# The pooling layer's first block without its sample and meta columns, and a new order of the first loads

## The chip, the cores and the metric

The kernel runs on the 8 cores of one Trainium2 chip. Each core computes one of the 8 prompts and 16 of the 128 samples, without talking to the others. The metric is the device time of the slowest core in microseconds, as the median of several runs.

## The reference, cut to what matters

One inference step of a 2-layer model with 1024 channels. A prompt has 16 meta tokens and 2048 prompt tokens; a sample has one new token and stored state.

```python
for i in range(DEPTH):                       # 2 layers
    xn = rmsnorm(h, norm_mix[i])
    if i % 2 == 0:
        mix, buf = multiscale_pool_mix(xn, pool_prev, w_pool, pool_scale)
    else:
        mix, s = retention_mix(xn, ...)
    h = h + mix
    h = h + swiglu(rmsnorm(h, norm_ffn[i]), w_gate, w_up, w_down)
```

The pooling mixer has four groups of 256 channels with trailing windows of 2, 4, 8 and 16 tokens. For each token it takes the mean of the normed rows in the window (fewer at the sequence's start), subtracts the token's own normed row, multiplies by a 256x256 matrix of its group and scales each channel. For a sample the window reaches into 15 stored normed rows (`state_pool`); the last 15 rows are also an output.

## The kernel before, in words

Channels lie on the 128 partitions, in 8 channel tiles; tokens are columns. The first part of the program works on tile A with NA = 1056 columns: 16 samples (columns 0 to 15), 16 meta tokens (16 to 31) and 1024 prompt tokens. The other 1024 prompt columns are tile B and come later. The FFN computes on blocks of BW = 352 columns; `FIRST` cuts the first of these in two, so the pooling layer on A has four blocks: b = 0 (columns 0 to 175), 1 (176 to 351), 2 (352 to 703) and 3 (704 to 1055). Their four loads from `xT` are called x0 to x3 below (the list `xl`).

Each block of the pooling layer goes through these functions:

- `p0_norm(b)`: squares of 8 channel tiles (ScalarE, VectorE, GpSimd), summed by 8 matmuls with ones into the bank `sx`, then two ScalarE steps give 1/root (`rstd`, `rms_root`).
- `p0_x(b)`: VectorE writes the normed columns, as bf16 in tile B's room for channel tiles 0 to 5, as float32 in the room of the rotation tables (`XF`, in `cs_sb`) for tiles 6 and 7.
- `p0_group(b, g)`: pool minus token. For windows 2, 4 and 8 by matmuls that add shifted columns with scaled identities (`snb`), copied out by ScalarE; for window 16 by GpSimd additions in `cs_sb` and one VectorE operation each. Block 0 does this from column 32 on only.
- `p0_out(b, g)`: the 256x256 matmuls (`hB`, `wring`), VectorE's scaled addition onto tile A (`hadd`), and ScalarE's squares for the FFN's norm.
- `p0_f(b)`: the norm ahead of the FFN into `xn`.

`p0_meta` computes pool minus token of the meta columns on GpSimd. `p0_sample` sums the stored rows (`PV`, in tile C's room, named `hC` in the rows) by 32 float32 matmuls of 16 columns into the bank `po`, copies the sum to `prevsum`, and writes the samples' pool minus token. Both write columns that block 0's `p0_out` reads: in the kernel before, all 176 columns of block 0 go through it together.

The order on each engine is not the order of the source. Every call only enters an operation with what it depends on and an estimated cost into one list for the whole program. `Prog.arrange` then plans: it simulates the five engines with these costs and one shared transfer line, tries some 20 sets of priorities (8 of them with random changes from a fixed seed), and takes the order with the smallest simulated end. The source order enters through the dependencies, through which ring buffer an operation gets, and as a small part of the first priorities. The estimates that matter here: a float32 matmul counts 4 passes of at least 64 columns, a transfer has 300 bytes per ns and 3 us for landing. The chip runs each engine's list strictly in order, with waits on semaphores; a transfer issued by SyncE (`sp`) or GpSimd (`pool`) stands in that engine's list, and its `after` list makes the engine wait until those transfers have landed.

The weights go through a ring `wring` by transfers that GpSimd issues: number 0 is the pooling matrices, 1 to 4 are the first four FFN tiles (`w_gu`). `gate` gives the transfers that must have landed before weight 1, 2, 3 and 4 is issued. The FFN's first three weight tiles are used together, block by block (`n_outer=3`).

`nps_prev` copies 14 of the 15 stored rows of each sample from one DRAM tensor to an output. `cf2` is a part of the constants that only the retention layer reads.

## Time and profile before

| what | value |
|---|---|
| time, median of 3 runs | 1647.43 us (1644.41 to 1648.02) |
| the profiled execution | 1646.35 us |
| its span, slowest core (core 7) | 1644.7 us |
| spans of all cores | 1629.8 to 1644.7 us |
| TensorE busy | 1581.0 us (96%) |
| VectorE, ScalarE, GpSimd busy | 885.0, 665.3, 610.2 us |

All rows and stretches are of core 7. PE is TensorE's matmuls, PEld its weight loads, DVE is VectorE, ACT ScalarE, POOL GpSimd, SP SyncE. L721 is the line of the matmul helper, L730 that of tensor-tensor operations, L733 of scalar-tensor-tensor ones, L741 of activations: one line stands for many places, so the tile names tell them apart. The granted clock (PEclk) is a share of TensorE's full 2.4 GHz.

### The profile page before, as it was taken

How to read it: one execution, taken by the hardware profiler on the slowest of the kernel's cores; microseconds unless marked ns; L12 is line 12 of the kernel's file. 1: busy time of each engine (PE TensorE's matmuls, PEld its weight loads, DVE VectorE, ACT ScalarE, POOL GpSimd, SP SyncE). 2: the span in 40 equal slices, each digit the busy share in tenths (PEclk: the TensorE clock that was granted, in tenths of full speed). 3: DMA queues.
4: the chain of work that ended last, by engine and by line, in shares of the span. 5: the costliest groups of instructions: out<-in, count | busy, mean ns of one | idle time of the engine just before them, and what ended most of it. 6: DMA issues, size and time to landing. Idle time of an engine off the chain costs nothing.

```text
span 1644.7 us, 32433 instructions; the slowest of 8 cores (1629.8 to 1644.7 us)
## 1 busy us (share of the span) xinstructions
PE 1581.0 (96%) x10775; PEld 1002.9 (61%) x10775; DVE 885.0 (54%) x1650; ACT 665.3 (40%) x1174; POOL 610.2 (37%) x921
## 2 busy tenths in 40 slices
PE   5899999999999998999999999999999999999996
PEld 4666666555565555666666666665555655666665
DVE  4822222855656782888374444576567657422225
ACT  5511022354433763444374535465454445220124
POOL 5300002557847671222140111134588578000014
PEclk9999999999999999999999999999999999999998
DMA  8544344243236568475769998967533331544413
GB/s 211 107 70 86 68 75 77 52 78 65 51 66 142 106 179 211 103 180 148 169 163 222 219 246 222 222 177 216 152 73 78 78 65 27 116 78 79 80 35 105
DMA packets 55746, 201.30 MB, mean 122 GB/s; under 512 B 6688, under 2 KB 21024, under 8 KB 45840
## 3 DMA queue, kind: packets, MB, share of 16 engines
q0 software_dynamic: 15840, 103.82, 37.4%
q1 hardware_dynamic: 39600, 95.07, 17.1%
q8 instruction: 90, 1.47, 0.4%
q14 instruction: 72, 0.59, 0.1%
q10 hardware_dynamic: 144, 0.35, 0.1%
HBM read 256.69 MB, written 47.25 MB: 185 GB/s over the span
## 4 chain that ended last, share of the span: by engine, by line
PE 85%; DMA 5%; DVE 3%; POOL 2%; issue 2%; ACT 1%; DVEq 0%; SPq 0%; POOLq 0%; ACTq 0%
PE pb L721 77%; PE po L721 3%; DMA nrs<-U 2%; DMA U<-sret 2%; PE psU L721 2%; PE sx L721 2%; PE sx L725 1%; DMA hC<-sp_prev 1%; PE psU L1299 1%; POOL accb L730 0%; DVE U L733 0%; DVE hB L733 0%; PE po L1337 0%; POOL aff L730 0%; ACT L741 0%
## 5 line engine op out<-in xcount | busy, mean ns | idle before, releaser
L721 PE MATMUL pb<-xn,wring 128*128 128x352 bf16 (+3 forms) x5856 | 914.8, 308 | 14.5 <-DVE hC L730 7.9
L721 PEld LDWEIGHTS pb<-xn,wring 128*128 128x128 bf16 x5856 | 562.4, 98 | 308.1 <-issue 28.3
L721 PE MATMUL pb<-hC,wring 128*128 128x352 bf16 (+4 forms) x2576 | 411.3, 305 | 2.1 <-DVE hB L730 1.9
L730 DVE TENSOR_TENSOR hC<-pb,sg 128x352 bf16<-128x352 f32 (+3 forms) x270 | 136.3, 508 | 352.1 <-PE pb L721 341.9
L721 PEld LDWEIGHTS pb<-hC,wring 128*128 128x128 bf16 x2576 | 245.7, 98 | 123.6 <-issue 8.9
L741 ACT ACTIVATE sg<-pb 128x352 bf16<-128x352 f32 (+3 forms) x270 | 120.6, 451 | 471.7 <-PE pb L721 454.8
L721 PE MATMUL pb<-wring,xn 128*128 128x512 bf16 (+1 forms) x544 | 155.1, 379 | 0.0
L157 POOL DMA_DIRECT2D wring<-w_gu x44 | 24.6, 560 | 313.3 <-PE pb L721 311.3
L730 POOL TENSOR_TENSOR accb<-accb,sq 128x352 f32<-128x352 f32 (+2 forms) x108 | 94.4, 874 | 81.1 <-ACT sq L741 57.4
L730 DVE TENSOR_TENSOR hB<-pb,hB 128x352 f32<-128x352 f32 (+4 forms) x152 | 73.3, 494 | 81.2 <-PE pb L721 79.1
L730 DVE TENSOR_TENSOR hA<-pb,hA 128x352 f32<-128x352 f32 (+1 forms) x144 | 72.4, 512 | 68.8 <-PE pb L721 68.3
L733 DVE SCALAR_TENSOR_TENSOR U<-psU,ksf,U 128x512 f32<-128x512 f32 x120 | 88.4, 746 | 23.1 <-DMA U<-sret 15.3
L733 DVE SCALAR_TENSOR_TENSOR U<-U,psU 128x1024 f32<-128x1024 f32 x64 | 78.0, 1218 | 24.2 <-PE psU L721 13.1
L1240 ACT ACTIVATE on<-po,stt 128x512 bf16<-128x512 f32 x68 | 52.9, 777 | 94.2 <-POOL stt L1234 47.2
L157 POOL DMA_DIRECT2D wring<-w_d x32 | 17.3, 541 | 187.8 <-PE pb L721 187.6
L730 POOL TENSOR_TENSOR aff<-aff,cf_sb 128x512 f32<-128x512 f32 (+1 forms) x68 | 67.5, 993 | 47.3 <-DVE aff L730 47.1
L737 ACT CAST U<-U 128x1024 bf16<-128x1024 f32 x64 | 66.7, 1043 | 36.5 <-DVE U L733 26.6
L737 ACT CAST snb<-U 128x1024 bf16<-128x1024 f32 x60 | 62.2, 1039 | 46.8 <-DVE U L733 39.0
L721 PEld LDWEIGHTS pb<-wring,xn 128*128 128x128 bf16 (+1 forms) x544 | 51.2, 98 | 48.0 <-issue 6.7
L1229 DVE BATCH_NORM_STATS2 stt<-po 128x6 f32<-128x512 f32 x68 | 47.4, 697 | 41.4 <-PE po L721 21.4
L730 DVE TENSOR_TENSOR aff<-sx,cf_sb 128x512 f32<-128x512 bf16 (+1 forms) x80 | 46.9, 586 | 37.7 <-PE sx L725 18.4
L741 ACT ACTIVATE sq<-hB 128x352 bf16<-128x352 f32 (+2 forms) x98 | 46.4, 486 | 48.5 <-DVE hB L730 19.8
(155 smaller groups left out, 1680.1 us busy)
## 6 DMA issues: line engine op xcount, KB each, us to landing
wring<-w_gu POOLq DMA_DIRECT2D x44, 1024.0 KB, 10.5
U<-sret SPq DMA_DIRECT2D x60, 512.0 KB, 6.5
nrs<-U SPq DMA_DIRECT2D x60, 512.0 KB, 9.0
wring<-w_in POOLq DMA_DIRECT2D x24, 1024.0 KB, 10.5
wring<-w_d POOLq DMA_DIRECT2D x16, 768.0 KB, 9.0
wring<-w_d POOLq DMA_DIRECT2D x16, 640.0 KB, 11.1
wring<-w_out POOLq DMA_DIRECT2D x8, 1024.0 KB, 10.0
hA<-xT SPq DMA_DIRECT2D x2, 1408.0 KB, 14.8
```

Source lines behind the costliest of these rows:

```text
L157: h.dma_start(out=o_ap, in_=i_ap).then_inc(sem, 16)
L721: return P.op('pe', lambda h: h.matmul(out, lhsT=lhsT, rhs=rhs, start=start, stop=stop), reads=reads, writes=writes, cost=passes * max(_fr ...
L725: return P.op('pe', lambda h: h.transpose(out, in_, ident), reads=reads, writes=writes, cost=max(_free(out), 64) / 2.4 + 1.3)
L730: return P.op(eng, lambda h: h.tensor_tensor(out=out, in0=a, in1=b, op=op), reads=reads, writes=writes, cost=cost)
L733: return P.op('dve', lambda h: h.scalar_tensor_tensor(out=out, in0=a, scalar=s, in1=b, op0=op0, op1=op1), reads=reads, writes=writes, cost ...
L737: return P.op('act', lambda h: h.copy(out=out, in_=in_), reads=reads, writes=writes, cost=130 + 0.93 * _free(out))
L741: return P.op('act', lambda h: h.activation(out=out, in_=in_, func=func, bias=bias, scale=scale), reads=reads, writes=writes, cost=160 + 0 ...
L1229: dve(lambda h: h.bn_stats(out=s[0:n, 0:6], in_=po[0:n, :]), [pok], [sk], 690)
L1240: act(lambda h: h.activation(out=on[0:n, :], in_=po[0:n, :], func=ACT.Identity, bias=s[0:n, 9:10], scale=s[0:n, 8:9]), [pok, sk], [onk], 777)
L1299: ins = e.matmul(psU[:, i, :], lhsT=identb[p, 32 * i + b + i:32 * i + b + i + 1].to_broadcast([32, 128]), rhs=vx[h][p, :], start=True, sto ...
```

## The change

Block 0's `p0_out` leaves out columns 0 to 31. A new function `p0_late` treats them for all 8 channel tiles together, once the sample and meta parts are there. The blocks' source order becomes norm, next norm, block, with the sample part, the late columns and the FFN's norms of blocks 0 and 1 behind block 1. The stored rows are loaded behind x1's landing and not ahead of x1, x3 behind x2's landing; weight 1 waits for the stored rows, weight 2 for x3, weights 3 and 4 for weights 1 and 2. The second part of the constants and the copy `nps_prev` follow the rotation tables' load. One `rstd` (block 2's) lives in `accb`, as four are held at once.

```diff
         xl = [load_x(A, FIRST[0][0], *FIRST[0])]
-        pvl = P.dma('sp', [(PV[:, 0, :], sp_prev[0:128, :]), (PV[0:112, 1, :], sp_prev[128:240, :])], writes=pvk, semkey='pv')
         xl.append(load_x(A, FIRST[1][0], *FIRST[1]))
-        xl.extend([load_x(A, c0, c0, n, after=xl[0:1]) for (c0, n) in FIRST[2:]])
-        gate.update({1: xl[1:2], 2: xl[2:3], 3: xl[3:4], 4: xl[3:4]})
+        xl.append(load_x(A, FIRST[2][0], *FIRST[2], after=xl[0:1]))
+        pvl = P.dma('sp', [(PV[:, 0, :], sp_prev[0:128, :]), (PV[0:112, 1, :], sp_prev[128:240, :])], writes=pvk, semkey='pv',
+                    after=xl[1:2])
+        xl.append(load_x(A, FIRST[3][0], *FIRST[3], after=xl[2:3]))
+        gate.update({1: [pvl], 2: xl[3:4], 3: [1], 4: [2]})
         w_issue()
-        cf2l = P.dma('sp', [(cf[:, NCF1:NCF], cfd[:, NCF1:NCF])], writes=['cf2'], after=xl[3:4])
-        P.dma('sp', [(nps_prev[:, :, :], sp_prev.rearrange("(b j) d -> b j d", j=15)[:, 1:15, :])],
-              semkey='o_npsprev', is_out=True, after=[cf2l])
...
-            pw[b] = rms_stats(c0, n)
+            pw[b] = rms_stats(c0, n, buf=(accB[0], 'accb') if b == 2 else None)
...
         def p0_sample():
-            nrows(xs[:], ['xs'], 0, 0)
...
+        def p0_late(wp, wk):
+
+            pb, pk = PO.take()
+            for cm in range(8):
+                g, m = cm // 2, cm % 2
+                for kc in range(2):
+                    mm(pb[:, cm * 32:(cm + 1) * 32], wp[:, g, kc, m * 128:(m + 1) * 128], B.b(2 * g + kc, 1, 0, 32), kc == 0, kc == 1,
+                       wk + B.bk(2 * g + kc, 1, 0, 32), [pk])
+            tmp = aff[:].rearrange("p a b -> p (a b)")[:, 0:256].rearrange("p (c n) -> p c n", c=8)
+            ak = [k for c in range(8) for k in A.fk(c, 0, 32)]
+            h32 = A.f3()[:, 0:8, 0:32]
+            tt('dve', tmp, pb[:, 0:256].rearrange("p (c n) -> p c n", c=8), bc_n(cf[:, C_PS:C_PS + 8], 32), ALU.mult,
+               [pk, 'cf'], ['aff'])
+            PO.free()
+            tt('dve', h32, h32, tmp, ALU.add, ak + ['aff'], ak)
+            aact(xn[:, 0:8, 0:32], h32, ACT.Square, ak, [k for c in range(8) for k in xk(c, 0, 32)])
+
         def p0_out(b, g, wp, wk):
             c0, n = FIRST[b]
+            if b == 0:
+                c0, n = 32, n - 32
...
         p0_norm(0)
+        nrows(xs[:], ['xs'], 0, 0)
         p0_meta()
+        p0_norm(1)
+        p0_block(0)
+        p0_norm(2)
+        p0_block(1)
+        p0_norm(3)
         p0_sample()
-        for b in range(last + 1):
-            if b < last:
-                p0_norm(b + 1)
-            else:
-                nrows(halo[:], [('halo', c) for c in range(8)], 1040, last)
-            p0_block(b)
-            if b < last:
-                p0_f(b)
-            else:
-                norm_soon(A, C_NF0, b, FIRST[b][0], FIRST[b][1], 'F00')
+        p0_late(wp, wk)
+        p0_f(0)
+        p0_f(1)
+        p0_block(2)
+        nrows(halo[:], [('halo', c) for c in range(8)], 1040, last)
+        p0_block(3)
+        p0_f(2)
+        norm_soon(A, C_NF0, last, FIRST[last][0], FIRST[last][1], 'F00')
         wrel(wprec)
-        P.dma('sp', [(cs[:, 0, :], csd[0, :, 0:NA]), (cs[:, 1, :], csd[1, :, 0:NA])], writes=csk, semkey='cs')
+        csl = P.dma('sp', [(cs[:, 0, :], csd[0, :, 0:NA]), (cs[:, 1, :], csd[1, :, 0:NA])], writes=csk, semkey='cs')
+        cf2l = P.dma('sp', [(cf[:, NCF1:NCF], cfd[:, NCF1:NCF])], writes=['cf2'], after=[csl])
+        P.dma('sp', [(nps_prev[:, :, :], sp_prev.rearrange("(b j) d -> b j d", j=15)[:, 1:15, :])],
+              semkey='o_npsprev', is_out=True, after=[cf2l])
```

## Rows read from the trace of the kernel before

**Rows 1.** The page's first part: busy time, share of the span, instructions.
```profile
PE 1581.0 (96%) x10775; PEld 1002.9 (61%) x10775; DVE 885.0 (54%) x1650; ACT 665.3 (40%) x1174; POOL 610.2 (37%) x921
```

**Rows 2.** Stretches of the span: length, each engine's busy time, granted clock, transfers.
```profile
0.00:80.00 80.00, 56.83 (x448) 42.38 (x448) 53.35 (x115) 44.50 (x120) 40.09 (x79) 0.96 0.76 163
80.00:400.00 320.00, 318.70 (x2090) 200.27 (x2091) 129.71 (x238) 84.40 (x163) 89.00 (x122) 1.00 0.39 69
```

**Rows 3.** Stretches inside the first 81 us; columns PE, PEld, DVE, ACT, POOL.
```profile
9.40:16.40 7.00, 1.33 (x8) 0.84 (x8) 4.49 (x11) 2.52 (x9) 3.39 (x6) 1.00 1.02 233
16.40:24.80 8.40, 8.03 (x43) 8.06 (x44) 0.00 (x0) 0.96 (x5) 3.21 (x11) 1.00 1.03 332
24.80:66.40 41.60, 34.92 (x242) 21.45 (x240) 39.41 (x80) 31.28 (x87) 29.10 (x47) 0.92 0.85 148
...
67.60:80.80 13.20, 11.34 (x147) 10.99 (x145) 8.72 (x21) 6.61 (x15) 0.00 (x0) 1.00 0.18 66
```

**Rows 4.** Timelines of TensorE, then ScalarE: start, length, idle before and releaser.
```profile
16.77 6.98 PE L721 MATMUL po<-cf_sb,hC 128*128 128x16 f32 x32 [4.85 <-DMA hC<-sp_prev]
...
62.92 0.46 PE L721 MATMUL pb<-xn,wring 128*128 128x176 bf16 x4
...
67.62 8.60 PE L721 MATMUL pb<-xn,wring 128*128 128x176 bf16 x111
...
23.84 0.27 ACT L737 COPY prevsum<-po 128x128 f32<-128x128 f32 x1 [10.97 <-PE po L721]
24.00 1.78 ACT L741 ACTIVATE xn<-hA 128x176 bf16<-128x176 f32 x7
```

**Rows 5.** Timeline of VectorE.
```profile
24.81 0.98 DVE L733 SCALAR_TENSOR_TENSOR hB<-prevsum,xs 128x32 bf16<-128x32 f32 x4 [8.48 <-POOL prevsum L730]
26.77 0.77 DVE L733 SCALAR_TENSOR_TENSOR hA<-pb,cf_sb,hA 128x176 f32<-128x176 f32 x2 [0.97 <-PE sx L721]
27.78 0.40 DVE L733 SCALAR_TENSOR_TENSOR hB<-hA,w,rstd 128x176 bf16<-128x176 f32 x1 [0.24 <-ACT rstd L741]
```

**Rows 6.** The chain of work that ended last, in order of time.
```profile
2.17 14.36 DMA hC<-sp_prev
```

**Rows 7.** Stretches of 2 us, columns as in rows 2.
```profile
38.00:40.00 2.00, 0.00 (x0) 0.00 (x0) 2.00 (x6) 1.53 (x6) 2.00 (x4) 1.00 1.44 266
...
46.00:48.00 2.00, 2.00 (x8) 1.03 (x7) 2.00 (x4) 0.85 (x2) 0.94 (x1) 0.50 1.01 164
```

**Rows 8.** First loads: kind, median to landing; x1's issue; x2's and x3's.
```profile
wring<-wpool POOLq DMA_DIRECT2D x1, 512.0 KB, 13.0
...
L157 SPq DMA_DIRECT2D hA<-xT x1: 1039/1039/1039, 2.6 to 2.6; - x1
...
DMA to landing us min/median/max: 15.7/15.7/15.7
...
L157 SPq DMA_DIRECT2D hA<-xT x2: 1723/3320/4917, 9.5 to 11.3; - x2
...
DMA to landing us min/median/max: 13.6/14.8/16.0
```

**Rows 9.** Groups by shape on VectorE: count, busy us, mean ns, idle before.
```profile
L733 DVE SCALAR_TENSOR_TENSOR hA<-pb,cf_sb,hA 128x176 f32<-128x176 f32 x16 | 5.8, 392 | 1.0 <-PE sx L721 1.0
...
L730 DVE TENSOR_TENSOR qm<-qsf,cf_sb 128x256 bf16<-128x256 f32 x8 | 4.3, 541 | 0.3
```

**Rows 10.** Weights 1 and 2 to 4, issued by GpSimd: starts, us to landing.
```profile
L157 POOL DMA_DIRECT2D wring<-w_gu x1: 596/596/596, 27.9 to 27.9; - x1
...
DMA to landing us min/median/max: 17.9/17.9/17.9
...
L157 POOL DMA_DIRECT2D wring<-w_gu x3: 535/550/591, 39.0 to 40.1; - x3
...
DMA to landing us min/median/max: 15.3/19.2/24.3
```

**Rows 11.** Timeline of SyncE: the rotation tables' issue.
```profile
64.23 0.82 SPq L157 DMA_DIRECT2D cs_sb<-cs  x2
```

More of the change, by code:

```diff
@@ L805, in square, with rms_root @@
             return o, ok
-        def rms_root(pb, pk, n):
-            r, rk = rstdR.next()
+        def rms_root(pb, pk, n, buf=None):
+            r, rk = buf if buf else rstdR.next()
             first = aact(r[:, 0:n], pb[:, 0:n], ACT.Ln, [pk, 'epsb'], [rk], bias=epsb[:, 0:1])
@@ L830, in last_sum, with rms_stats @@
             tt('pool', out, x[0], x[1], ALU.add, x[2], outk)
-        def rms_stats(c0, n, tiles=range(8)):
+        def rms_stats(c0, n, tiles=range(8), buf=None):
             bank = SX
@@ L836, in rms_stats @@
                 mm(pb[:, 0:n], onesb[:], xn[:, c, c0:c0 + n], c == tiles[0], c == tiles[-1], ['onesb'] + xk(c, c0, n), [pk])
-            out = rms_root(pb, pk, n)
+            out = rms_root(pb, pk, n, buf)
             bank.free()
```

## The prediction

> **What bounds the kernel now.** I read the page first. TensorE is busy 96% of the span [rows 1], so the change can only give back what TensorE loses. The stretches show where that is: 23.2 us idle in the first 80, and 63.7 - 23.2 = 40.5 us spread over the other 1564.7 [rows 1, 2]. The change lies wholly in the first stretch, and the next 320 us have only 1.3 us to spare.
>
> Next I read the engines' timelines through the first 80 us, to see which engine sets the pace. From 24.8 to 66.4 us VectorE is busy 39.4 of 41.6 us while TensorE has gaps [rows 3]: there the pooling layer runs at VectorE's pace. From 16.4 to 24.8 us VectorE does nothing. The reason is on two other timelines. The sample part's 32 float32 matmuls wait 4.85 us for the stored rows and run 16.77 to 23.75 us; every pooling matmul of block 0 stands behind them in TensorE's list. ScalarE waits 10.97 us for the same matmuls to copy their result, and the squares of block 1 stand behind that copy [rows 4, 5]. The chain that ended last agrees: it begins with 14.36 us of the stored rows' transfer and goes on through the float32 matmuls [rows 6].
>
> So there are two things to lose in this stretch: a VectorE gap of 8.48 us before the sample's small operation at 24.81, and then nearly two more until block 0's first output addition at 26.77 [rows 5].
>
> A caution on the clock: after TensorE had 0.00 busy from 38 to 40 us, the granted clock reads 0.50 in three stretches of 2 us up to 48, TensorE's 1.2 GHz level; the last of them stands in the rows. But VectorE is busy 2.00 of 2.00 us there [rows 7], so the low clock has cover and I price its removal at nothing. If that cover went, half of the 6 us, 3 us, would be to gain.
>
> **Part 1: block 0 without the sample and meta columns.** Its output additions no longer wait for the sample matmuls or GpSimd's meta sums. Block 0's normed columns end on VectorE where its gap begins, at 24.81 - 8.48 = 16.33 [rows 5]. The pooling weights are in at 1.9 + 13.0 = 14.9 us [rows 8]. TensorE waits idle for the stored rows up to 16.77 [rows 4], so block 0's outputs can follow the normed columns directly. Eight of them at 392 ns [rows 9] are 3.1 us: VectorE is then at about 19.5 at the latest, in place of a start of these additions at 26.77.
>
> **Part 2: the stored rows behind block 1's and block 2's columns.** Landing times: x1 was issued at 2.6 and landed 15.7 later, at 18.3. x2 and x3 were issued at 9.5 and 11.3 and landed 13.6 and 16.0 later, at 23.1 and 27.3 [rows 8]. The stored rows are 0.98 MB ahead of x1; at the 233 GB/s of 9.4 to 16.4 us [rows 3] that is 4.2 us, so x1 lands at about 14. From its first square at 24.00 to its first normed column at 27.78 block 1 took 3.8 us [rows 4, 5]. These columns can begin at 18, while block 0's additions end, against 27.78 before. x2 now goes ahead of the stored rows and lands near 19; they land near 22; x3, issued when x2 has landed, comes in near 27 as before, because the bytes before it are the same. So x2 is there 4 us earlier than before, and block 2's work stands behind all of block 1's.
>
> Here a rule speaks against the change. The trace first: the same link moved 332 GB/s from 16.4 to 24.8 with all loads queued behind one another [rows 3]; the new waits issue the stored rows after x1 has landed and x3 after x2. If nothing else is in flight, each such wait empties the link. The Trainium skill (DMA: Bandwidth & Descriptors, "Anatomy of one DMA") gives each transfer a fixed part of about 2 us, mostly the receipt before the semaphore moves. By it two waits would cost 4 us of the link if nothing overlapped. The rows show the cover: by the landing times above x2 is in flight during the first wait and the stored rows during the second, so I price both at nothing. An x3 at 31 would still be ahead of its use, as some 14 us of VectorE work on block 1's and block 2's columns and block 0's norm lie between 18 and it.
>
> **Part 3: what is added.** `p0_late` puts two operations of 128x256 on VectorE, at most 541 ns each by the nearest row [rows 9], together 1.1 us; block 0's eight additions lose 32 of their 176 columns each, at most 8 x 392 x 32/176 = 0.6 us back, and as an operation has a fixed part I take half. Net +0.8 us on VectorE. Its 16 matmuls of 32 columns and one Square of 256 lie on engines with gaps: nothing. Using `accb` for one root and moving the sample's normed rows on GpSimd cost nothing, as GpSimd is busy 29.1 of 41.6 us [rows 3].
>
> **Part 4: the float32 matmuls in their new place.** They are still 7.0 us of TensorE, 218 ns each [rows 4], and now stand in the stretch where VectorE is full. The planner's cost for one is 4 x 64/2.4 + 1.3 = 108 ns, so it takes them for 3.5 us: up to 3.5 us are not planned for. Lower bound 0: VectorE has normed columns to make meanwhile. Upper bound 7.0, if VectorE runs dry for all of it. I take 2, nearer to 0, because block 1's eight normed columns alone are about 3 us of VectorE work that needs no matmul.
>
> **Part 5: later loads and gates.** The constants and the stored rows' copy to the output leave the time of the first weights' loads and follow the rotation tables, issued at 64.23 [rows 11]. The link is then at 66 GB/s [rows 3], while 0.5 + 0.9 MB no longer compete with the weights. Weight 1 landed at 27.9 + 17.9 = 45.8 us, weight 2 at 39.0 + 15.3 = 54.3 and weight 3 near 39.6 + 19.2 = 58.8 us [rows 10], and the first FFN matmul ran at 62.92 [rows 4]. With 1.4 MB less and a start some 6 us earlier they can be in by 53 to 57: enough for an FFN start at 57. On SyncE nothing but those two transfers waits behind the tables; the sync queue is empty for that time. I price it at nothing. The gate of weight 3 on weight 1, however, is a wait in GpSimd's list; behind it stand the window sums of channels 6 and 7, and behind these VectorE and TensorE.
>
> **The sum.** Gap removed 8.5 us, additions +0.8, float32 block +2: 5.7 us, and I round to 6. Nothing downstream absorbs it: from 67.6 to 80.8 TensorE is busy 11.3 of 13.2 us, and from 80 to 400 it is 318.7 of 320 [rows 2, 3], so what comes earlier stays earlier. The profiled execution took 1646.35 us (span 1644.7 and 1.65 around it), 1.1 under the median of 1647.43. So its like would be 1640.4 and the median 1641.4.
>
> **Rivals.**
> *A, a late weight takes the gap's place (slower).* Weight 3 may be issued only when weight 1 has landed, weight 4 when weight 2 has. Before, three issues went out together from 39.0 to 40.1. If weight 1 goes at 28 as before and takes its 17.9 us, weight 3 goes at 46 and, with 15 to 24 us to land [rows 10], arrives at 61 to 70. Above 63 us it decides: the FFN starts later than before. At 67 the kernel would be 4 us slower, 1651. Against it: the first one's 17.9 us were shared with loads that are moved away. The planner's own belief of 10 us for a weight, though, makes a stall of the GpSimd list possible. Chance 0.16.
>
> *B, TensorE's gaps fill too.* With weights in by 45, block 0's 96 FFN matmuls (7.4 us, by 111 of them in 8.60 us [rows 4]) could run in gaps, of which TensorE has 6.7 us from 24.8 to 66.4 [rows 3]. If most of them fill, some 6 us more are gained: 1635.5. For it: no low clock from idle time either. Against: the VectorE product and ScalarE's table loads come along. Chance 0.16.
>
> *C, it makes no difference.* The gap moves: TensorE's float32 block starves VectorE for the full 7.0 us, leaving 8.5 - 0.8 - 7.0 = 0.7 us; or the order is planned anew over the whole program and returns the gain, somewhere in the 40 us that TensorE idles after 80. Time 1646.7. Chance 0.18.
>
> The remaining 0.50 is the forecast, 1641.4, its own range 1638.5 to 1644.
>
> **From this to the numbers.** A difference of 0.2%, 3.3 us, is what a measurement of this kernel can tell from none. Faster: forecast (0.45 of its 0.50), B 0.16 and a little of C, 0.63. Same: most of C and edges, 0.20. Slower: A, and a new order that is worse elsewhere, 0.17. The range reaches to B's time with the float32 block at its lower bound, 1634, and to A's with a smaller stall, 1650.
>
> **What will show it.** Right, if VectorE's gap from 16.3 to 24.8 shrinks to under 2 us, block 0's additions begin before 18, the float32 matmuls stand after 21, the first FFN matmul comes before 58 and VectorE's dense stretch ends near 61. Wrong in part 2, if the squares of block 1 begin after 17. Rival A shows as TensorE or GpSimd waiting on a weight; C as a VectorE gap beside the float32 matmuls, or TensorE idle time after 80 us grown by 3 us or more; B as more than 8 us less idle before 80. The prediction fails if a different engine than VectorE sets the pace from 25 to 60 us.

## The result, and the profile after

The changed kernel took 1655.34 us (median of 7 runs; the kernel before 1647.43 us on the same chip). The ratio is 1.0046, 95% interval 1.0035 to 1.0057: 0.46% or some 8 us slower, where 6 us faster was forecast. In some executions of every version the cores of a die show a lower granted clock and the time is 1 to 17% longer; medians here are over all executions, ratios leave these out. The profiled execution has core 5 as its slowest, with a span of 1653.8 us.

The page's first part after, for [rows 1]:

```profile
PE 1584.7 (96%) x10791; PEld 1005.9 (61%) x10791; DVE 884.3 (53%) x1652; ACT 665.9 (40%) x1175; POOL 610.4 (37%) x921
```

Stretches of core 5 after, for [rows 2]:

```profile
0.00:80.00 80.00, 54.17 (x432) 40.58 (x432) 50.98 (x113) 43.32 (x117) 40.71 (x79) 0.98 0.68 159
80.00:400.00 320.00, 317.38 (x2085) 200.79 (x2085) 127.79 (x237) 83.21 (x160) 84.79 (x118) 0.99 0.35 68
400.00:600.00 200.00, 198.65 (x1319) 118.74 (x1318) 126.46 (x229) 98.51 (x164) 133.58 (x198) 1.00 0.47 108
600.00:660.00 60.00, 54.88 (x357) 34.75 (x355) 31.97 (x52) 31.00 (x56) 19.65 (x31) 0.94 0.80 196
660.00:1000.00 340.00, 333.49 (x2312) 215.35 (x2311) 217.49 (x409) 154.02 (x238) 78.70 (x135) 1.00 0.75 183
1000.00:1200.00 200.00, 193.80 (x1281) 116.49 (x1279) 117.41 (x217) 104.83 (x158) 66.63 (x97) 0.99 0.74 184
```

The same stretches of core 7 before, behind its first two, which are [rows 2]:

```profile
400.00:600.00 200.00, 197.27 (x1311) 117.55 (x1310) 129.11 (x234) 97.63 (x165) 132.94 (x196) 1.00 0.50 105
600.00:660.00 60.00, 51.31 (x334) 32.78 (x332) 26.14 (x44) 27.73 (x51) 17.40 (x28) 0.94 0.88 199
660.00:1000.00 340.00, 333.80 (x2312) 214.80 (x2309) 214.37 (x404) 154.37 (x239) 78.56 (x135) 1.00 0.73 179
1000.00:1200.00 200.00, 197.17 (x1315) 120.03 (x1316) 119.77 (x220) 106.26 (x161) 66.39 (x95) 1.00 0.79 199
```

Take TensorE's idle time in each (length less busy). Up to 1000 us it is 23.2 + 1.3 + 2.7 + 8.7 + 6.2 = 42.1 us before and 25.8 + 2.6 + 1.4 + 5.1 + 6.5 = 41.4 us after. The matmuls done by then are 6,495 and 6,505, of which 16 are `p0_late`'s. So the two are level at 1000 us, although the changed stretch is the first 80. The difference shows from there on: 2.8 against 6.2 us of idle time in the next 200, where the change touches no operation.

**What stands in that place.** VectorE's timeline on core 5 after:

```profile
1118.44 1.59 DVE L733 SCALAR_TENSOR_TENSOR U<-psU,ksf,U 128x512 f32<-128x512 f32 x2
1124.92 1.61 DVE L733 SCALAR_TENSOR_TENSOR U<-psU,ksf,U 128x512 f32<-128x512 f32 x2 [4.88 <-DMA U<-sret]
1126.44 0.95 DVE L730 TENSOR_TENSOR hA<-pb,cs_sb 128x352 f32<-128x352 f32 x2
```

TensorE's, of the same time:

```profile
1121.36 1.89 PE L721 MATMUL pb<-wring,xn 128*128 128x512 bf16 x8
1127.54 3.57 PE L721 MATMUL pb<-wring,xn 128*128 128x512 bf16 x8 [4.28 <-DVE hA L730]
```

And stretches of 4 us (columns as in rows 2):

```profile
1124.00:1128.00 4.00, 0.46 (x2) 0.22 (x3) 2.98 (x5) 1.29 (x2) 0.90 (x2) 0.95 0.52 182
1128.00:1132.00 4.00, 4.00 (x15) 1.33 (x14) 4.00 (x7) 1.53 (x3) 2.21 (x4) 0.63 0.87 308
```

`U<-psU,ksf,U` updates a sample's retention state, which SyncE has loaded from `sret`. The load is late, VectorE waits 4.88 us in front of it, and the products `hA<-pb,cs_sb` that TensorE's banks wait for stand behind it in VectorE's list. TensorE loses 4.28 us, then the granted clock reads 0.63 over 4 us, and eight matmuls take 3.57 us where eight alike had just taken 1.89. SyncE's waits of 1095 to 1150 us tell why the load is late:

```profile
SPq L357 <- ACT U L741: 33.2, 8, 10.0
SPq L357 <- DMA nrs<-U: 22.4, 5, 13.9
```

Each state buffer goes load, update, store, load. The next load waits for the store of the state before it (`nrs<-U`), and the store for ScalarE's last step on it. In the kernel before (core 7) SyncE waits there too, but its longest wait for a store is 5.7 us and not 13.9, and VectorE never waits for `sret`:

```profile
SPq L357 <- DMA nrs<-U: 18.0, 5, 5.7
```

On the other cores after, VectorE's wait near 1120 us is 3.4 (core 0), 1.0 (3) and 3.0 us (7) and none is listed on the rest. Core 3, with a span of 1652.1 us, meets the same chain at its next place (VectorE's timeline, TensorE's, and a stretch of 4 us):

```profile
1165.73 0.29 DVE L730 TENSOR_TENSOR U<-sx,cf_sb 128x128 bf16<-128x128 f32 x1 [5.16 <-DMA nrs<-U]
```
```profile
1166.17 0.58 PE L721 MATMUL po<-hC,U 128*128 128x512 bf16 x1 [4.49 <-DVE U L730]
```
```profile
1164.00:1168.00 4.00, 1.83 (x8) 1.00 (x9) 0.29 (x1) 0.47 (x1) 2.20 (x4) 0.50 0.32 122
```

**The last matmuls.** TensorE's waits there, first after, then before:

```profile
1637.21 1.13 PE L721 MATMUL pb<-hC,wring 128*128 128x160 bf16 x14 [1.96 <-DVE hB L730]
1638.53 1.96 PE L721 MATMUL pb<-hC,wring 128*128 128x160 bf16 x26 [0.19 <-DVE hB L730]
```
```profile
1628.21 3.21 PE L721 MATMUL pb<-hC,wring 128*128 128x160 bf16 x40 [1.20 <-DVE hB L730]
```

Another 0.8 + 0.2 us is lost there, and on cores with a low clock behind that gap more. The first gap is 1.96 or 1.97 us on all eight cores after, and 1.20 to 1.22 on all eight before.

**The start.** VectorE's timeline after, for [rows 5]:

```profile
12.22 1.13 DVE L730 TENSOR_TENSOR xn<-hA 128x176 bf16<-128x176 f32 x3 [5.81 <-DMA hA<-xT]
15.13 0.88 DVE L733 SCALAR_TENSOR_TENSOR cs_sb<-hA,w,rstd 128x160 f32<-128x160 f32 x2 [1.79 <-ACT rstd L741]
...
24.01 0.64 DVE L733 SCALAR_TENSOR_TENSOR hA<-pb,cf_sb,hA 128x144 f32<-128x144 f32 x2 [3.02 <-POOL cs_sb L730]
...
34.55 0.40 DVE L733 SCALAR_TENSOR_TENSOR hA<-pb,cf_sb,hA 128x176 f32<-128x176 f32 x1 [5.45 <-PE pb L721]
```

TensorE's, for [rows 4]:

```profile
22.83 0.84 PE L721 MATMUL sx<-xn,onesb 128*128 128x352 bf16 x2 [4.12 <-ACT xn L741]
...
26.64 0.44 PE L721 MATMUL po<-cf_sb,hC 128*128 128x16 f32 x2
...
34.46 1.41 PE L721 MATMUL po<-cf_sb,hC 128*128 128x16 f32 x8
...
66.52 0.24 PE L721 MATMUL pb<-xn,wring 128*128 128x176 bf16 x1
```

ScalarE's, where x2 is waited for:

```profile
22.19 0.88 ACT L741 ACTIVATE xn<-hA 128x352 bf16<-128x352 f32 x2 [3.02 <-DMA hA<-xT]
22.98 0.80 ACT L737 CAST hB<-pb 128x144 bf16<-128x144 f32 x4
```

The loads, for [rows 8] and [rows 10], each line of issues above its time to landing: x2 alone, the stored rows, weights 2 to 4:

```profile
L157 SPq DMA_DIRECT2D hA<-xT x1: 368/368/368, 12.2 to 12.2; - x1
...
DMA to landing us min/median/max: 9.9/9.9/9.9
...
L157 SPq DMA_DIRECT2D hC<-sp_prev x2: 341/546/751, 14.5 to 14.9; - x2
...
DMA to landing us min/median/max: 9.6/10.2/10.8
...
L157 POOL DMA_DIRECT2D wring<-w_gu x3: 591/591/591, 43.3 to 56.3; - x3
...
DMA to landing us min/median/max: 7.9/9.2/11.5
```

The gap of 8.48 us at 16.3 is gone, as forecast; three take its place, at 21 us (3.02), at 29 us (5.45) and 5.81 instead of 3.32 us in front of the first squares. The profile names GpSimd for the one at 21 us; the product that VectorE needs there begins on TensorE only at 23.49, behind block 2's sums (the row at 22.83). In the stretch that was VectorE's dense one, it is now busy 32.55 us and not 39.41:

```profile
24.80:66.40 41.60, 34.69 (x238) 24.21 (x236) 32.55 (x67) 24.87 (x69) 26.44 (x43) 0.96 0.66 135
```

The first FFN matmul is at 66.52 us on this core, against 61.66 on the same core before. Over the eight cores it stands at 60.4 to 67.0 us (61.2 to 63.9 before): three cores are 1.6 to 3.4 us earlier, three 4.5 to 5.8 us later, two level. No core has the 57 us that was forecast.

**Slow and fast neighbours.** The same core number is not the same case in two executions. In 197 of the 229 executions that enter the ratios of this document, the four longest spans belong to one core of each pair of neighbours (0 and 1, 2 and 3, 4 and 5, 6 and 7). In the profile before these are 1, 2, 4 and 7, and x0 lands later on them from the start: VectorE's first squares begin at 9.5 to 11.6 us there and at 8.5 to 8.8 on the others. Core 5 was the faster of its pair before and is the slower one after. By this sorting the first FFN matmul comes at 62.9 to 63.9 us on the slower cores before and at 62.6 to 67.0 after, on the faster ones at 61.2 to 62.0 and 60.4 to 63.5. What the two cores of a pair share was not tested.

### The profile page after: what moved, and what is told of

It is laid out like the page before. It is cut to its first block, busy times and chain, and to the rows that moved or that the text cites. A ratio compares the mean times of both kernels' runs of the same rounds, so it can differ in the third digit from the quotient of the medians.

```text
span 1653.8 us, 32463 instructions; the slowest of 8 cores (1636.1 to 1653.8 us)
## 1 busy us (share of the span) xinstructions
PE 1584.7 (96%) x10791; PEld 1005.9 (61%) x10791; DVE 884.3 (53%) x1652; ACT 665.9 (40%) x1175; POOL 610.4 (37%) x921
## 4 chain that ended last, share of the span: by engine, by line
PE 82%; DMA 7%; DVE 3%; POOL 3%; issue 2%; ACT 2%; DVEq 0%; POOLq 0%; SPq 0%; ACTq 0%
PE pb L721 74%; DMA U<-sret 3%; PE po L721 3%; DMA nrs<-U 3%; PE psU L721 2%; PE sx L721 1%; PE sx L725 1%; DMA hA<-xT 1%; DVE xn L733 1%; PE psU L1316 0%; ACT on L1257 0%; POOL aff L730 0%; DVE U L733 0%; DVE hA L730 0%; DVE hB L733 0%
## 5 line engine op out<-in xcount | busy, mean ns | idle before, releaser
L721 PEld LDWEIGHTS pb<-hC,wring 128*128 128x128 bf16 x2576 | 246.0, 98 | 126.2 <-issue 11.5
L721 PE MATMUL pb<-wring,xn 128*128 128x512 bf16 (+1 forms) x544 | 161.3, 383 | 4.7 <-DVE hA L730 4.3
L730 POOL TENSOR_TENSOR accb<-accb,sq 128x352 f32<-128x352 f32 (+2 forms) x108 | 93.6, 866 | 60.2 <-ACT sq L741 40.9
L721 PEld LDWEIGHTS pb<-wring,xn 128*128 128x128 bf16 (+1 forms) x544 | 51.9, 98 | 55.9 <-issue 13.1
L721 PE MATMUL pb<-hB,wring 128*128 128x352 bf16 (+3 forms) x256 | 60.7, 309 | 4.5 <-DVE hA L733 3.2
L741 ACT ACTIVATE U<-U 128x1024 f32<-128x1024 f32 x60 | 63.1, 1055 | 4.0
## 6 DMA issues: line engine op xcount, KB each, us to landing
wring<-w_d POOLq DMA_DIRECT2D x16, 640.0 KB, 10.8
```

The source lines that it names most:

```text
L721: return P.op('pe', lambda h: h.matmul(out, lhsT=lhsT, rhs=rhs, start=start, stop=stop), reads=reads, writes=writes, cost=passes * max(_fr ...
L730: return P.op(eng, lambda h: h.tensor_tensor(out=out, in0=a, in1=b, op=op), reads=reads, writes=writes, cost=cost)
L741: return P.op('act', lambda h: h.activation(out=out, in_=in_, func=func, bias=bias, scale=scale), reads=reads, writes=writes, cost=160 + 0 ...
```

## The experiments

The start is what the change edits. The 13,961 operations from the first FFN on are the same in both kernels, but `arrange` plans both parts in one go, and it put them in another order: 3,797 of TensorE's 10,367 places, 462 of VectorE's 1,546, 278 of ScalarE's 1,038 and 45 of SyncE's 168 differ. On these last three engines most lie in the FFN of tile B (operations 7103 to 9256 of the common ones) and the second retention layer (9257 to 11947), where the stall was found; of TensorE's, 1,382 lie ahead of 7103. So the first pair swaps these orders. The form of all such kernels: `arrange` is run as it is, and then, on each engine, the places of the common operations from LO to HI are filled with these operations in the donor's order (`TAIL`, whose unpacking is left out here; LO is 0 and HI 13961 in the first pair).

```diff
-        for i in best[1]:
-            self.ops[ops[i].eng].append(ops[i])
+        n0 = n - 13961
+        lists = [[i for i in best[1] if self.eng[i] == e] for e in range(len(ENGS))]
+        for e, mine in enumerate(TAIL):
+            it = iter([i for i in mine if LO <= i < HI])
+            lists[e] = [next(it) + n0 if LO <= i - n0 < HI else i for i in lists[e]]
```

**e1_new_start_old_rest**: the changed kernel, common operations in the order of the kernel before.

> The changed kernel in its first 561 operations (the whole pooling layer's source), but every engine runs the 13961 operations behind them in the order of the kernel before. Theory 'two losses' (the start loses some 4 us, the order planned anew for the rest loses another 4): 1651, about +0.25%. Theory 'the start alone': as the changed kernel, 1655. Theory 'the order alone': 1647 or below. In the profile of the slowest core the first FFN matmul stays at 65 to 67 us in any case.

**e2_old_start_new_rest**: the kernel before, common operations in the changed kernel's order.

> The mirror image: the first 542 operations of the kernel before in their old order, and behind them the changed kernel's order of the common 13961. Theory 'two losses': 1651. 'The start alone': 1647.4, no change. 'The order alone': 1655.

Measured: e1 0.9992 (0.998 to 1.0004), 1647.94 us; e2 1.0059 (1.0036 to 1.0081), 1657.74 us. The loss goes with the order, and the start without it is worth nothing that can be measured.

**e5_new_but_second_half** and **e6_new_but_first_half**: the changed kernel with the old order for common operations 7103 to 13960 alone, and for 0 to 7102 alone.

> The changed kernel, but the operations from the second half's first FFN on (source positions 7103 to 13961 of the common part) stand in the old kernel's order among themselves; everything ahead of them keeps the new order. Theory 'the second half's order costs the time, by a state load that VectorE waits for in front of the rotation products near 1120 us': within 0.15% of the kernel before. Rival 'the loss is spread over the whole of the new order': half of it, +0.25%.

> The complement: the changed kernel with the first half's operations behind the start (positions 0 to 7103) in the old order, the second half in the new one. Theory 'second half': slower by 0.4 to 0.6%, as the changed kernel. Rival 'spread': +0.25%. In the profile VectorE should wait some 5 us for a state load near 1120 us.

Measured: e5 1.0001 (0.999 to 1.0011), e6 1.0039 (1.0027 to 1.0052). The order of the second half carries it; TensorE's 1,382 other places in the first half cost nothing that can be measured.

**e7_old_start_seed3** and **e8_new_start_seed3**: is it the change that makes the planner's order bad, or is it luck? Only the seed of the planner's random priorities is altered, in the kernel before (e7) and in the changed one (e8).

```diff
-        rng = np.random.default_rng(1)
+        rng = np.random.default_rng(3)
```

> The kernel before, nothing changed but the seed of the planner's random tries (3 in place of 1). The order that comes out for the common part differs from the changed kernel's in only some 150 places, and from its own old one in some 4700. Theory 'the measured loss has nothing to do with what the change does, the planner just settled on its other order': +0.5%, 1655. Rival 'the loss comes from the new start': no change.

> The changed kernel with the planner's seed 3: a third order, unlike both. If the choice of order is a matter of luck of some 0.5%, this falls anywhere from -0.2 to +0.6% against the kernel before; the state-load wait near 1120 us decides which. If the start were what costs, it would be at +0.46% as the changed kernel.

Measured: e7 1.0055 (1.0042 to 1.0068), 1657.46 us; e8 0.9998 (0.9988 to 1.0008), 1648.80 us. e7 is the unchanged kernel. Its new plan differs from the changed kernel's in only some 150 places, and it has the same loss and the same mark in VectorE's waits of 1095 to 1150 us:

```profile
DVE U L733 <- DMA U<-sret: 5.4, 1, 5.4
DVE hA L730 <- PE pb L721: 3.0, 3, 2.2
```

e6 has the first at 6.1 and e2 at 5.9 us on their slowest cores; e1 and e5 have none there. e8's plan is a third order, unlike both (7,094 of TensorE's places differ from the changed kernel's, 6,956 from the old ones), and as good as the old one. So the slow order comes with the old start too, and a good one with the new start.

The planner itself gives simulated ends of 1583.8 us for the kernel before, 1587.6 for the changed one, 1585.3 for e7 and 1583.5 for e8. In the changed kernel and in e7 the order taken is one that its fixed turns reach before any random try, and no random try beat it. In the kernel before and in e8 a random try did. So the good order of the kernel before was a find of the random tries, and the changed kernel fell back to the other kind. The planner ranks these four as the chip does, but sees 0.1 to 0.3% between the kinds where the chip shows 0.5%.

**e3_f32_cost**: e1, with the planner told twice the time for a float32 matmul.

```diff
-            passes = 4 if rhs.dtype == F32 else 1
+            passes = 8 if rhs.dtype == F32 else 1
```

> As the first of these, but the planner is told that a float32 matmul of 16 columns takes 215 ns (8 passes in its formula) and not 108; it plans the pooling layer anew, the rest keeps the old order. Theory 'the float32 block starves VectorE, because it is planned at half its length': VectorE's gap of 5.45 us among block 0's and block 1's additions falls below 3 us and the time to about 3 us under the first of these. Rival 'the late loads set the start': within 1.5 us of it.

**e4_old_loads**: e1, with the first loads and gates of the kernel before; the constants and the copy stay late.

```diff
         xl = [load_x(A, FIRST[0][0], *FIRST[0])]
+        pvl = P.dma('sp', [(PV[:, 0, :], ...), (PV[0:112, 1, :], ...)], writes=pvk, semkey='pv')
         xl.append(load_x(A, FIRST[1][0], *FIRST[1]))
-        xl.append(load_x(A, FIRST[2][0], *FIRST[2], after=xl[0:1]))
-        pvl = P.dma('sp', [(PV[:, 0, :], ...), (PV[0:112, 1, :], ...)], writes=pvk, semkey='pv', after=xl[1:2])
-        xl.append(load_x(A, FIRST[3][0], *FIRST[3], after=xl[2:3]))
-        gate.update({1: [pvl], 2: xl[3:4], 3: [1], 4: [2]})
+        xl.extend([load_x(A, c0, c0, n, after=xl[0:1]) for (c0, n) in FIRST[2:]])
+        gate.update({1: xl[1:2], 2: xl[2:3], 3: xl[3:4], 4: xl[3:4]})
```

> As the first of these, but with the loads in the order of the kernel before: stored rows between x0 and x1, x2 and x3 behind x0's landing, the weights' gates as before; the two late transfers stay late. The new source order of the blocks stays. Theory 'x1 right behind x0 shares the link with it, and the stored rows share it with x2': x0 lands near 9.5 us again in place of 10.6 to 12.2, and the time is 2 to 4 us under the first of these. Rival 'the float32 block alone': no change against it. What I predicted for the change, 6 us under the kernel before, would show here if the loads alone spoiled it: 1641.

Measured: e3 0.9995 (0.9981 to 1.0009), e4 1.0029 (1.0015 to 1.0043). A truer cost of the float32 matmuls brings nothing in time, although VectorE's gap at 29 us shrinks from 5.44 us on e1's slowest core to 1.45 on e3's. The new loads are worth something: without them the new source order is 0.3% slower than before, with them level (the planner orders the start anew in e4, so this is the loads together with their plan). The first FFN matmul of e4 stands at 65.3 to 68.0 us on all cores. Block 1's normed columns then stand behind the float32 matmuls (VectorE's timeline of e4):

```profile
22.97 2.29 DVE L874 SCALAR_TENSOR_TENSOR hB<-hA,w,rstd 128x176 bf16<-128x176 f32 x4 [4.32 <-PE po L862]
```

**e10_no_f32_block**: e1, with the 32 float32 matmuls replaced by one bf16 matmul of 128 columns with the same wait for the stored rows. It leaves out the sums over the stored rows.

```diff
-            for c in range(8):
-                g = c // 2
-                for kc, kn in ((0, 128), (1, 112)):
-                    off = C_AW + (kc * 4 + g) * 16
-                    mm(pb[:, c * 16:(c + 1) * 16], PV[0:kn, kc, c * 128:(c + 1) * 128], cf[0:kn, off:off + 16],
-                       kc == 0, kc == 1, pvk + ['cf'], [pk])
+            mm(pb[:, 0:128], onesb[:], identb[:], True, True, pvk + ["onesb", "identb"], [pk])
```

> New start, old order behind it, and the 32 float32 matmuls over the stored rows are replaced by one bfloat16 matmul of 128 columns with the same wait for the stored rows: the sums over the stored rows are left out. It shows what the block costs in the start, and whether time saved there reaches the end. Theory 'the block starves VectorE by some 5 us': the first FFN matmuls come 4 to 6 us earlier than with the block, and the time falls by the same, to 1643. Rival 'a stretch paced by the state transfers, near 640 us, takes up what the start gives': the start is earlier, the time within 2 us of the one with the block. Rival 'the block is hidden': neither.

Measured: 1.0000 (0.9974 to 1.0027). The first FFN matmul comes at 59.7 to 61.4 us on all cores, where e1 has 60.4 to 67.8: on three cores some 6 us are gained at the start, and the time doesn't show them. Carried to the end, 6 us under e1 would be 0.9956, outside the interval; a part of up to 3 us would lie inside it.

**e11_x1_behind_x0**: e1, with x1 issued once x0 has landed.

```diff
-        xl.append(load_x(A, FIRST[1][0], *FIRST[1]))
+        xl.append(load_x(A, FIRST[1][0], *FIRST[1], after=xl[0:1]))
```

> New start, old order behind it, and x1 is issued only when x0 has landed, so that x0 has the queue alone. Theory 'x1 right behind x0 shares the link and makes x0 2 us late': x0 lands at 8 to 9.5 us in place of 10.6 to 12.2, block 0's normed columns come 2 us earlier, and the time falls by 1 to 2 us or not at all, if x1's own lateness takes it back. Rival 'x0 is late for another reason': it lands where it did.

Measured: 0.9988 (0.9975 to 1.0001). x0 did not land earlier for it: VectorE's first squares start at 10.9 to 13.2 us on the cores, in e1 at 10.9 to 12.4, before at 8.5 to 11.6. That x0 is slowed by x1 beside it has fallen. What does go with x0 is where GpSimd's list has the pooling matrices' load (`wring<-wpool`). In the kernel before and in e2 it is issued at 1.95 us, and the squares begin at 8.5 to 11.6 us. In e7, where SyncE's first loads are the same and in the same order, the plan has it ahead of two small memory fills, at 1.59 us, and the squares begin at 10.2 to 14.4; so it is in the changed kernel and in e4 (1.56 us; 10.8 to 13.1 and 11.0 to 12.6). The first line is of before, the second of e7:

```profile
1.94 0.71 POOL L157 DMA_DIRECT2D wring<-wpool  x1 [0.42 <-issue]
```
```profile
1.59 0.71 POOL L157 DMA_DIRECT2D wring<-wpool  x1 [0.33 <-issue]
```

No run moves this load alone, so that it is the cause is not shown.

**e9_one_step_later**: the changed kernel's own order, with the state update in front of which VectorE waited, its TensorE and ScalarE parts and its load moved by hand to where the old order has them, behind the rotation's products.

```diff
-        for i in best[1]:
-            self.ops[ops[i].eng].append(ops[i])
+        lists = [[i for i in best[1] if self.eng[i] == e] for e in range(len(ENGS))]
+        n0 = n - 13961
+        for e, who, behind in ((0, (9092,), 9340), (0, (9284,), 9465), (2, (9093, 9094, 9095, 9096), 9329),
+                               (1, (9136, 9137, 9188, 9189), 9420), (4, (9091,), 9090)):
+            l = [i for i in lists[e] if i - n0 not in who]
+            at = l.index(behind + n0) + 1
+            lists[e] = l[:at] + [i + n0 for i in who] + l[at:]
```

> The changed kernel as it was planned, but one pair of sample steps is moved to where the old order has it: two broadcasts on TensorE, four state updates on VectorE, their four copies on ScalarE, and one state load ahead of two stores on SyncE, all to behind the rotation products of the same head. Nothing else moves. Theory 'VectorE stands for a state load in front of the rotation products, and that costs': the wait of up to 4.9 us near 1120 us is gone and the time falls by 3 to 6 us against the changed kernel, to 1649 to 1652. Rival 'the wait is only a symptom, the state transfers are late all through the new order': it comes back at the next load, 1655.

Measured: 1.0080 (1.0063 to 1.0098), slower still. The wait near 1120 us shrank to 0.3 to 1.7 us, on seven cores, and came back at the next place: TensorE waits 5.4 to 6.5 us for VectorE there on every core. VectorE's waits on e9's core 3 from 1150 to 1200 us:

```profile
DVE U L737 <- DMA nrs<-U: 6.8, 1, 6.8
```

**e12_new_short_stores** and **e13_old_rest_short_stores**: the stores of the sample states of heads 2 and 3 move 128 of 1024 columns, in the changed kernel with its own order (e12) and in e1 (e13). The planner is told the full size, so the orders stay. Both leave out the rest of these stores.

```diff
-                    P.dma('sp', [(nrs[b, h], t)], reads=k, semkey=('sst', i), is_out=True)
+                    m = 1024 if u < 32 else 128
+                    P.dma('sp', [(nrs[b, h][:, 0:m], t[:, 0:m])], reads=k, semkey=('sst', i), is_out=True).cost = 524288
```

> The changed kernel's own order, but the sample states of heads 2 and 3 are stored only in their first 128 of 1024 columns: 32 of 64 stores move an eighth of their bytes, and the rest of these outputs is left out. Theory 'the new order of the second half runs short of transfer time there': VectorE's wait for a state load near 1120 us goes and the loss with it, to 1647 or less. Rival 'the new order costs compute time of its own': still slower than the next kernel by 6 us or more.

> New start, old order behind it, with the same short stores. Theory 'transfer time': no more than 2 us under the kernel with full stores (1648), so that the two orders come within 2 us of each other. Rival 'compute': the distance between the orders stays at 7 us.

Measured: e12 1.0036 (1.0022 to 1.005), e13 0.9997 (0.9983 to 1.0012). VectorE's wait for `sret` is gone on every core of e12 (0.2 us at most), yet e12 stays 0.39% behind e13. TensorE's busy time from 1000 to 1300 us tells how much came back; one line each of before (core 7), e1 (core 4), after (core 5), e7 (core 3) and e12 (core 2), their slowest cores:

```profile
1000.00:1300.00 300.00, 295.34 (x1987) 179.23 (x1988) 188.14 (x348) 151.63 (x232) 142.81 (x210) 1.00 0.61 151
```
```profile
1000.00:1300.00 300.00, 294.39 (x1980) 178.37 (x1979) 187.87 (x347) 151.32 (x233) 142.61 (x209) 1.00 0.60 150
```
```profile
1000.00:1300.00 300.00, 290.25 (x1937) 174.44 (x1935) 180.11 (x334) 148.57 (x229) 138.56 (x204) 0.99 0.61 147
```
```profile
1000.00:1300.00 300.00, 284.53 (x1884) 170.10 (x1883) 174.56 (x324) 144.91 (x224) 138.42 (x202) 0.98 0.60 144
```
```profile
1000.00:1300.00 300.00, 293.32 (x1971) 177.59 (x1970) 182.68 (x339) 149.54 (x230) 139.52 (x207) 1.00 0.50 114
```

Idle: 4.7 and 5.6 us with the old order, 9.8 and 15.5 with the new one, 6.7 with the new one and short stores. So the state transfers are most of what core 5 loses in this stretch, and e12 loses in other places. VectorE's lists tell where. From its last operation among the common ones up to 6300 to its last among those up to 11947, e12 takes 573.7 to 574.0 us on all eight cores, where e13 takes 571.9 to 572.1 on seven (and the changed kernel 574.6 to 580.8). So 1.8 us stay whatever the stores move. From there to the end of the span e12 takes 243.7 to 244.0 us on six cores and e13 241.6 on all: another 2.1. Of the end, e12's core 2 has the gap of after and then a low clock (26 matmuls in 3.50 us, in 1.96 after):

```profile
1635.11 1.13 PE L844 MATMUL pb<-hC,wring 128*128 128x160 bf16 x14 [1.97 <-DVE hB L853]
1636.42 3.50 PE L844 MATMUL pb<-hC,wring 128*128 128x160 bf16 x26 [0.19 <-DVE hB L853]
```

**e14_old_ffn** and **e15_old_ret**: the changed kernel with the old order for common operations 7103 to 9099 alone, and from 9100 on alone.

> The changed kernel with the operations 7103 to 9100 of the common part (the second half's first FFN and the state steps among it, up to head 2) in the old order. Theory 'the loss is made in this FFN, where the state transfers fall behind': within 0.15% of the kernel before. Rival 'it is made in the retention part behind it': +0.4%.

> The complement: operations 9100 to 13961 (the second retention part and the last FFN) in the old order, all else the changed kernel's. Theory 'the FFN': +0.4%. Rival 'the retention part': within 0.15% of the kernel before.

Measured: e14 1.0070 (1.0054 to 1.0086); e15 1.0058 (1.0036 to 1.0080), from two executions only. Both theories fell: neither half of the good order takes the loss away, and e14 is slower than the changed kernel (1.0046). The loss can't be put down to one of the halves. That an order's FFN part and its retention part belong together would fit; it is not shown.

**e16_both**: e1 with the edits of e3 and e11.

> The changed start with the operations behind it in the order of the kernel before, x1 issued once x0 has landed, and the planner told 8 passes for a float32 matmul. The theory that the order behind the start carries the loss, and that the start's own gain is absorbed near 600 us: the two edits each measured 0.9988 and 0.9995 of the kernel before, so together 0.998 to 0.9995, about 1645 us. The rival, that the float32 block and the gaps of the start still cost VectorE some us that would count: 0.996 or lower, under 1641 us. If the first FFN matmul comes earlier than in the start-only run on the slow cores and the time stays, the first theory holds again.

Measured: 0.9984 (0.9974 to 0.9994), 1645.35 us against 1648.67. The first FFN matmul is at 60.2 to 62.0 us on all cores, so no core is late any more. It is the only one of the sixteen experiments whose interval lies wholly under 1: 2.6 us, at the edge of what can be told, and under the 3.3 us that the prediction itself asks for.

## Why the prediction was wrong, point by point

**The step that failed** is the sum's "Nothing downstream absorbs it [...] so what comes earlier stays earlier", for two reasons. The larger: the order of the rest was taken as given. Rival C named a new plan for the whole program, but let it do no more than return the gain, and "a new order that is worse elsewhere" shared 0.17 with rival A, which alone had 0.16. The new plan measured 1.0046 - 0.9992 = 0.54%, or 8.9 us (e1 against after), and 0.55% with no change of the start at all (e7). A mechanism that moves a third of TensorE's list deserved a range of its own, on both sides.

The other reason: a lead or a lag at the start is evened out near 600 us. Up to 600 us TensorE idles 23.2 + 1.3 + 2.7 = 27.2 us before and 25.8 + 2.6 + 1.4 = 29.8 after; from 600 to 660 us it is 8.7 against 5.1. Before, one wait of TensorE behind `hC` holds 6.7 us of this, at the time when SyncE stores sample states and loads the next (TensorE's timeline before, then SyncE's waits from 590 to 680 us):

```profile
647.18 16.21 PE L721 MATMUL pb<-xn,wring 128*128 128x352 bf16 x94 [6.68 <-DVE hC L730]
```
```profile
SPq L357 <- DMA nrs<-U: 25.3, 3, 16.8
```

The cores drift apart in this place. VectorE's 1100th operation from the end starts at 573.3 to 576.0 us on the eight cores before, its 1000th from the end at 665.5 to 678.3. In e1, with the same order behind the start, the slowest core is 4.6 us behind the slowest one of before at the first of these (579.7 against 575.1) and 1.4 behind at the second (679.7 against 678.3). That e10's 6 us of start don't show in the time fits this. That the transfers are what evens it out was read from the rows and not tested by itself.

**A step ahead of it failed too.** The sum's first line, "Gap removed 8.5 us", did not hold: the gap went, and as much came back within the pooling layer. With the old order behind it (e1) the first FFN matmul stands at 60.4 to 67.8 us, against 61.2 to 63.9 before and 57 in the forecast. So the 6 us were at no time there to be kept, and the start alone measures 0.9992. Rival C forecast that outcome (1646.7 us) for the start.

**Bounds now.** The readings of TensorE's losses and of VectorE's pace in the first 80 us hold. But a gap given back there is a gain on one core's start and not yet one of the slowest core's end. In the kernel before the spans of the cores lie 15 us apart on the same work, so the end is set in places that the first 80 us don't show.

**Part 1.** The gap at 16.3 went, and block 0's additions start at 24.01, not before 18. Two things were missed. x0 landed at 12.2 us, not at 9.5: e11 excludes x1 beside it, and e7 points at the order of GpSimd's first operations. And the planner put two of block 2's squares ahead of block 0's casts in ScalarE's list, and their sums ahead of block 0's products in TensorE's, so that block 0 waits 3.02 us for x2. I had placed block 0 directly behind its normed columns, which no list promised.

**Part 2.** x1 at about 14: right (1.6 + 12.9 = 14.5). x2 near 19: 12.2 + 9.9 = 22.1. Stored rows near 22: 25.3. x3 near 27: 22.2 + 7.7 = 29.9. The last three are late by x0's 2.7 us and little more, so the links between them were sized well. Block 1's squares begin at 14.94 us, before the 17 that would have been wrong. The two waits cost nothing visible: x2 is in flight during the first and the stored rows during the second, as the issue and landing times above show. e11 has the other case, a wait with none of SyncE's loads in flight: on its core 5 the transfers fall to 38 GB/s from 10 to 12 us, where e1's core 5 has 198. The Trainium skill (DMA: Bandwidth & Descriptors, "Anatomy of one DMA") gives about 2 us as the fixed part of a transfer on GpSimd's path; the two waits here are SyncE's, and the trace has no 4 us for them. And e4 shows the sign: the new loads, with their plan, are worth 0.37% to the new source order.

**Part 3.** `p0_late`'s two VectorE operations took 0.42 us each, under the 0.54 allowed. Right and small.

**Part 4.** The float32 block was priced at 2 us between bounds of 0 and 7. VectorE's gap beside it is 5.45 us on core 5 and 2.26 on core 1: the bounds held, and the choice was low for the slow cores. e3 and e10 shrink it to 1.4 us on their slowest cores, and the time does not follow.

**Part 5 and rival A.** Weights 2 to 4 landed 7.9 to 11.5 us after their issue, against 15 to 24 before, and weight 3 (issued at 53.8) was in at 63.0, just at the limit named for rival A. TensorE has no wait on a weight there. The later loads cost nothing, as said; rival A did not come.

**Rival B** did not come: TensorE's idle time before 80 us grew from 23.2 to 25.8 us, three cores start the FFN later, and the earlier ones by 3.4 us at most. Of **rival C's** signs the gap beside the float32 block came; TensorE's idle time after 80 us grew from 40.5 to 43.3 us, just short of the 3 us named. Busy time after 80 us grew as well, by 6.4 us, some of it the low clock behind the stalls.

**Open.** Which operations of the slower order cost the 1.8 us that every core of e12 loses between the first half's end and the second retention layer's, and what the rest of e12's 0.39% against e13 (6.4 us, of which 3.9 are placed above) is. Whether the pooling matrices' earlier load is why x0 lands later. And what makes one core of a pair the slower one, now this one and now that.

## What to carry to other kernels

Where one planner orders the whole program, an edit of 80 us can redraw the other 1570, and that draw here is 0.5%, more than the edit's own worth. Before an edit is judged, hold the order of all untouched operations fixed, or plan both versions with a few seeds: e1 took one run to tell the edit (0.9992) from the plan (0.54%). A good time may itself rest on a lucky plan, as the kernel before's did. And before a gain at the start is counted, look for the first place downstream where the cores of the same kernel drift apart, as there something other than TensorE's list sets the time.

## What the runs showed of the hardware

A stall costs more than its length. Behind TensorE's 4.28 us of idle time the granted clock read 0.63 over 4 us (0.50 in the first 2, the 1.2 GHz level), and eight matmuls took 3.57 instead of 1.89 us: 1.7 us on top. On core 3 it read 0.50 over 4 us behind 4.49 us. At the end of e12, 26 matmuls took 3.50 us in place of 1.96.

A transfer issued alone lands sooner, but not in proportion: x2 took 9.9 us with the stored rows issued 2.3 us behind it, and 13.6 before with x3 beside it. The eight cores, with the same program and each its own data, differ by 15 and 18 us in span in the two profiles, and the slow ones change from execution to execution, but are mostly one of each pair of neighbours (197 of 229 executions; drawn at random it would be 16 of 70).
